# Sample attention and half of the conditioning slices moved into the output projection, two counts of the bit search moved to ScalarE

## The chip, the cores and the metric

One core of one Trainium2 chip runs the whole program. Its engines are TensorE (PE), VectorE (DVE), ScalarE (ACT), GpSimd (POOL) and SyncE (SP), which only issues DMAs. Each engine works through its own instructions in the order of the program and waits on semaphores for the others. The metric is the device time of one execution in microseconds (us), lower is better.

## The reference

One inference step of a two-layer decoder trunk on 1024 prompt tokens and 8 sequences of 4 sample tokens, T = 1056 columns of D = 1024 features. Layer 0 is sparse attention, layer 1 a short convolution; each has a SwiGLU feed-forward, and every sub-layer a norm whose shift, scale and gate come from a conditioning vector (`mod = silu(c) @ ada_w + ada_b`). What matters here:

```python
q, k, v, qi, ki, wi = attn_project(h, w_in, pos)          # 16 query heads, 4 key heads of 64
sc = indexer_scores(qi, wi, ki, valid)                    # one score per query token and key
_, sel = lax.top_k(sc, topk)                              # 256 keys (prompt), 129 (sample)
o = sparse_attend(q, take_rows(k, sel), take_rows(v, sel), valid)   # softmax over those alone
yp = yp + g1p * (o @ w_o)                                 # then norm 2 and the feed-forward
```

The sample tokens attend to 512 cached keys, read through a page table (4 pages of 128 for each sequence), and to their own 4.

## The kernel before

**Numbers.** Products are made to fp32 accuracy from three passes: a weight tile is split into `uhi` (ACT, `split_hi` L294, `proj_hi` L731) and `ulo` (POOL, `split_lo` L301, `proj_lo` L737), and `up_product` (L313, matmuls on L309) issues 24 matmuls for 128 output features and one chunk of CH = 352 columns; I call this an item. Three chunks cover T.

**Loads.** Weights come through `wraw`, a ring of WR = 4 slots of 512 KB, in one fixed order. SP issues them; each waits until the slot's last user is done (`ring_wait` L636).

**Stages.** (a) Norm 1, the indexer's projections, and the index scores for query tiles 2 to 7 of 128 tokens and for the sample (to 197.5 us); tile i sees 128 (i + 1) keys, so the rows of scores are 384 to 1024 long. (b) `pe_proj_b`, the other projections in 39 items, with rotations (`pe_rot` L747) and K and V turned to tokens (ACT L937). Into these items all 80 chunks of conditioning weights `ada_w` are woven: `pe_chunks` L754, matmuls on L765, a chunk being 512 KB, one ring slot; eight chunks make a slice, which ACT takes to `qstage` (L782) and `mod` (L788). In the meantime DVE runs `dve_select` (L1369): the k-th largest score of every row by a binary search over the 32 bits of a float. Each of 32 iterations counts, for six tiles and the sample, the scores at or over a candidate (`count`, L1383), and makes the next candidate with small steps in two groups (`small` L1416; L1419, L1421, L1423, L1425). (c) Sample attention, `pe_att_s` L1525 with its ACT, DVE and SP parts: eight batches in a software pipeline, K and V pages of a batch loaded by SP with a table read each (L1223 to L1233), keys turned (L1480), scores with mask (L1488, L1492), probabilities turned (L1500), values (L1514). DVE also makes the masks of the six tiles from the thresholds there (`dve_mask` L1455, seven instructions each, one of them a scan, L1466). (d) Prompt attention, `pe_att` L1662: 64 pairs of heads, tile by tile, three pairs ahead; PE scores L1629, DVE adds the mask and takes the extreme (L1686), ACT exponentiates (L1729), POOL scales (L1764), PE turns (L1640, L1645) and multiplies with the values (L1658), DVE and ACT copy. (e) Output section, `pe_out` L1807: 24 items with the gate and the residual added by DVE (L1868), and norm 2's sums of squares (`pe_add`, L345) and its application between them; then the feed-forward, whose first half units belong to the window shown below.

**SP's order around the change:** the stores of q, the 16 DMAs of output weights 0 to 3 (`sp_out_w`, L1782), the pages of the sample, the q tiles of prompt attention, then the reload of y (L1787, 4.2 MB) and the other output weights.

**PE's order** is the list of calls:

```python
            pe_proj_b(pe)
            pe_att_s(pe)
            pe_att(pe)
            pe_out(pe)
            pe_ffn(pe, "ffn0", 1, 2)
```

## Time and profile before

| | us |
|---|---|
| median of 3 runs | 2957.48 |
| lowest, highest | 2954.46, 2960.81 |
| the profiled execution | 2959.58 |
| its span in the trace | 2957.2 |
| (b) projections and selection | 257.0 |
| (c) sample attention | 108.4 |
| (d) prompt attention | 250.6 |
| (e) output section, with twelve half units of the feed-forward | 163.7 |

The four stages are windows of the trace, cut where PE's work changes; they touch, from 197.5 to 977.2 us. PE is busy for 2784.2 us of the span (94%), DVE for 1266.0, ACT for 788.4, POOL for 879.3. A row of windows gives for a stretch the busy time and the number of instructions of each engine, then TensorE's granted clock as a share of the full 2.4 GHz, the busy share of the DMA engines and what they moved. A row of a timeline gives start, duration, engine, line, operation, output and inputs; in square brackets the idle time ahead of it and what ended it. SPq stands for SP's issue of DMAs.

### The profile page before, as it was taken

How to read it: one execution, taken by the hardware profiler on the slowest of the kernel's cores; microseconds unless marked ns; L12 is line 12 of the kernel's file. 1: busy time of each engine (PE TensorE's matmuls, PEld its weight loads, DVE VectorE, ACT ScalarE, POOL GpSimd, SP SyncE). 2: the span in 40 equal slices, each digit the busy share in tenths (PEclk: the TensorE clock that was granted, in tenths of full speed). 3: DMA queues.
4: the chain of work that ended last, by engine and by line, in shares of the span. 5: the costliest groups of instructions: out<-in, count | busy, mean ns of one | idle time of the engine just before them, and what ended most of it. 6: DMA issues, size and time to landing. Idle time of an engine off the chain costs nothing.

```text
span 2957.2 us, 46842 instructions
## 1 busy us (share of the span) xinstructions
PE 2784.2 (94%) x18034; PEld 2529.6 (86%) x18034; DVE 1266.0 (43%) x3043; ACT 788.4 (27%) x1488; POOL 879.3 (30%) x673
## 2 busy tenths in 40 slices
PE   5878895999999999999999989999799999999999
PEld 4746673557798999999999889999699999999999
DVE  6499998556614222222223253323432222222233
ACT  4151212387616111111111441111331111111113
POOL 3312442133315322232222342222242223223320
PEclk8999996599999999999999999999899999999999
DMA  8216654200041111111111111012011221111101
GB/s 291 77 44 207 211 190 140 65 23 16 2 130 29 43 43 43 43 43 43 43 43 43 43 48 53 15 57 58 1 43 49 59 60 45 43 43 43 43 15 60
DMA packets 207293, 191.17 MB, mean 65 GB/s; under 512 B 32176, under 2 KB 185368, under 8 KB 206906
## 3 DMA queue, kind: packets, MB, share of 16 engines
q1 hardware_dynamic: 207162, 189.38, 21.4%
q8 instruction: 88, 1.44, 0.2%
q14 instruction: 43, 0.35, 0.0%
HBM read 173.86 MB, written 15.48 MB: 64 GB/s over the span
## 4 chain that ended last, share of the span: by engine, by line
PE 84%; SPq 3%; DVE 3%; POOL 3%; DMA 2%; ACT 2%; issue 2%; DVEq 0%; ACTq 0%; POOLq 0%
PE PS L309 69%; PE PS L1629 3%; PE PS L1658 3%; PE PS L1640 2%; PE PS L345 2%; DVE s_all L1343 1%; DMA wraw<-in_ada_w_dram 1%; PE PS L765 1%; SPq L676 1%; POOL ulo L301 1%; ACT na L418 1%; PE PS L2332 1%; POOL hlo L430 1%; DVE na L394 1%; SPq L675 1%
## 5 line engine op out<-in xcount | busy, mean ns | idle before, releaser
L309 PE MATMUL PS<-hhi,uhi 128*128 128x352 f32 (+1 forms) x3240 | 1065.3, 329 | 27.8 <-DVE hlo L1117 10.4
L309 PE MATMUL PS<-hhi,ulo 128*128 128x352 f32 (+1 forms) x3240 | 1047.4, 323 | 0.0
L309 PE MATMUL PS<-hlo,uhi 128*128 128x352 f32 (+1 forms) x3240 | 1046.7, 323 | 0.0
L309 PEld LDWEIGHTS PS<-hhi,uhi 128*128 128x128 f32 (+1 forms) x3240 | 612.8, 189 | 50.0 <-issue 28.4
L309 PEld LDWEIGHTS PS<-hlo,uhi 128*128 128x128 f32 (+1 forms) x3240 | 614.5, 190 | 3.5 <-issue 0.2
L309 PEld LDWEIGHTS PS<-hhi,ulo 128*128 128x128 f32 (+1 forms) x3240 | 613.1, 189 | 0.8
L309 PE MATMUL PS<-ahi,dhi 128*128 128x352 f32 x1248 | 424.3, 340 | 26.7 <-DVE y L478 21.5
L2030 POOL TENSOR_TENSOR alo<-af,ahi 128x352 fp32r<-128x352 f32 x132 | 125.1, 948 | 1073.4 <-ACT ahi L1975 1073.4
L2077 DVE TENSOR_TENSOR af<-sg,PS 128x352 f32<-128x352 f32 x132 | 68.8, 521 | 872.9 <-PE PS L309 857.6
L309 PE MATMUL PS<-ahi,dlo 128*128 128x352 f32 x1248 | 404.8, 324 | 0.0
L309 PE MATMUL PS<-alo,dhi 128*128 128x352 f32 x1248 | 403.5, 323 | 0.0
L478 DVE SCALAR_TENSOR_TENSOR y<-PS,mod,y 128x352 f32<-128x352 f32 x416 | 242.7, 584 | 177.0 <-PE PS L309 177.0
L301 POOL TENSOR_TENSOR ulo<-wraw,uhi 128x1024 fp32r<-128x1024 f32 x120 | 285.3, 2400 | 69.6 <-ACT uhi L294 69.5
L309 PEld LDWEIGHTS PS<-ahi,dhi 128*128 128x128 f32 x1248 | 235.6, 189 | 57.1 <-DVE y L487 23.9
L1973 ACT ACTIVATE sg<-PS 128x352 f32<-128x352 f32 x132 | 61.3, 464 | 678.4 <-PE PS L309 678.3
L309 PEld LDWEIGHTS PS<-alo,dhi 128*128 128x128 f32 x1248 | 236.7, 190 | 3.8 <-issue 0.7
L309 PEld LDWEIGHTS PS<-ahi,dlo 128*128 128x128 f32 x1248 | 236.4, 189 | 0.0
L1975 ACT ACTIVATE ahi<-af 128x352 fp32r<-128x352 f32 x132 | 65.8, 498 | 500.5 <-DVE af L2077 500.5
L1764 POOL TENSOR_SCALAR Pb<-Pb,bv 128x128 f32<-128x128 f32 (+7 forms) x128 | 93.7, 745 | 238.2 <-DVE bv L1693 238.2
L1383 DVE TENSOR_SCALAR_CACHE_REDUCE junkA<-s_all,bv 128x1024 bf16<-128x1024 f32 (+4 forms) x162 | 162.6, 1004 | 1.4 <-DVE bv L1410 0.3
L481 DVE SCALAR_TENSOR_TENSOR y<-PS,mod,y 128x320 f32<-128x320 f32 x208 | 114.5, 551 | 55.5 <-PE PS L309 47.1
L294 ACT ACTIVATE uhi<-wraw 128x1024 fp32r<-128x1024 f32 x120 | 119.7, 1045 | 55.8 <-PE PS L309 27.1
(261 smaller groups left out, 2848.0 us busy)
## 6 DMA issues: line engine op xcount, KB each, us to landing
wraw<-in_ffn_w_gu_dram SPq DMA_DIRECT2D x88, 512.0 KB, 7.3
wraw<-in_ada_w_dram SPq DMA_DIRECT2D x80, 512.0 KB, 4.7
draw<-in_ffn_w_down_dram SPq DMA_DIRECT2D x44, 512.0 KB, 4.3
wraw<-in_conv_w_in_dram SPq DMA_DIRECT2D x24, 512.0 KB, 7.1
adaw<-in_ada_w_dram SPq DMA_DIRECT2D x16, 512.0 KB, 12.6
y_scratch<-y SPq DMA_DIRECT2D x1, 4224.0 KB, 12.5
q_scratch<-kiB SPq DMA_DIRECT2D x24, 176.0 KB, 3.8
y<-y_scratch SPq DMA_DIRECT2D x1, 4224.0 KB, 13.2
```

The costliest lines, as they stand in the source:

```text
L294: act.activation(uhi[:, u % WR, :, 0:cols], wraw[:, slot, :, 0:cols], ACT.Copy).then_inc(up_hi, 1)
L301: pool.tensor_tensor(ulo[:, u % WR, :, 0:cols], wraw[:, slot, :, 0:cols], uhi[:, u % WR, :, 0:cols].bitcast(F32), ALU.subtract).then_inc(u ...
L309: last = pe.matmul(out, w(kt), x(kt), start=(n == 0), stop=(n == 3 * count - 1))
L478: dve.scalar_tensor_tensor(out=y[:, m, chunk(n)], in0=b[:, 0:CH], scalar=gate(m)[:, 0:1], in1=y[:, m, chunk(n)], op0=ALU.mult, op1=ALU.add ...
L481: dve.scalar_tensor_tensor(out=y[:, m, 2 * CH:SEQ], in0=b[:, 0:PC], scalar=gate(m)[:, 0:1], in1=y[:, m, 2 * CH:SEQ], op0=ALU.mult, op1=ALU ...
L1383: return dve.tensor_scalar(junk(j, rows, L), s, at, 0.0, ALU.is_ge, ALU.add, accum_out=one(cnt, j)[0:rows])
L1629: last = pe.matmul(wide(2 * g)[:, c], q_of(i)[64 * g:64 * g + 64, t, :], kT[64 * g:64 * g + 64, t // 4, c], start=True, stop=True)
L1658: last = pe.matmul(bank[6 + n % 2][64 * g:64 * g + 64, 0:P], v_tok[:, j, 64 * kv:64 * kv + 64], PT[:, n % 2, g, j * P:j * P + P], start=(j ...
L1764: pool.tensor_scalar(p, p, bv[:, at:at + 1], 1.0, ALU.mult, ALU.mult).then_inc(p_nrm, 1)
L1975: act.activation(ahi[:, jj, chunk(n)], af[:, p, :], ACT.Copy).then_inc(act_hi, 1)
L2030: pool.tensor_tensor(alo[:, jj, chunk(n)], af[:, k % 2, :], ahi[:, jj, chunk(n)].bitcast(F32), ALU.subtract)\
L2077: dve.tensor_tensor(af[:, p, :], sg[:, p, :], bank[2 * p + 1][:, 0:CH], ALU.mult).then_inc(act_f, 1)
```

## The change

1. **ACT counts tiles 7 and 6** (1024 and 896 scores a row) with Sign and a sum, in `act_count`, one iteration in each of the items 2 to 33, on semaphores `cand_rdy` and `sign_cnt`. DVE counts the other five and waits for `sign_cnt` ahead of the first small step. Because Sign sums +1, 0 and -1, a short refinement of the two thresholds follows the loop.
2. **40 of the 80 chunks** (`SG_W` = 5 slices of 10) stay in the projections; the gains that need the others are made behind the output section (`dve_gains_late`).
3. **Prompt attention follows the projections directly.** DVE makes the masks of the sample and of tile 2 first; the other five are cut in 30 steps, ahead of the pairs 0 to 27 (`dve_masks_at`). For tiles 0 to 3, q is loaded in two halves into free parts of `PT`. The splits of output weights 0 to 3 lie at pairs 6 to 19 on ACT and POOL.
4. **The output section is 20 slots and eight items.** The slots hold 16 items (none in slots 0, 5, 10, 15), the sample attention (batch c from slots 2c and 2c + 1 on, keys turned in two halves over one bank), 40 chunks in slots 0 to 14, and the output weights 4 to 7. K and V have two buffers in place of four. SP issues the pages of a batch in odd slots. y comes back in three parts. The last eight items take chunk 1 and 2 of the columns; for these the weights 0 to 3 are loaded and split again (`N_OUT` = 12). Items use two banks (the last eight four) in place of six.

In the diff's core, "..." marks what is left out:

```diff
-N_SG = ADA1 // 8
+N_SG, SG_W = ADA1 // 8, 5
...
 def chunk_at(item):
-    return ADA1 * item // N_ITEMS
+    return 8 * SG_W * item // N_ITEMS
+
+
+def slot_chunks(s):
+
+    sg, r = divmod(s, 3)
+    lo = 8 * (SG_W + sg) + 3 * r
+    return range(lo, min(lo + 3, 8 * (SG_W + sg) + 8)) if s < 15 else range(0)
+
+
+TURN_AT = {4: 0, 6: 1, 10: 2, 12: 3, 16: 4}
...
+        def act_count(act, item):
+
+            i = item - 2
+            if not 0 <= i < 32:
+                return
+            act.wait_ge(cand_rdy, i + 1)
+            for j in range(NA):
+                L = L_OF[(7, 6)[j]]
+                act.activation(junkA[:, SEQ * j:SEQ * j + L], score((7, 6)[j]), ACT.Sign, bias=bv[:, CAND + j:CAND + j + 1],
+                               scale=-1.0, accum_out=bv[:, BS + j:BS + j + 1]).then_inc(sign_cnt, 1)
...
+        def sp_keys(sp, b):
+            sp.wait_ge(tpb_mm if b < 2 else kst_mm, turned_b(60, 1) if b < 2 else 2 * b - 2)
+            for g in range(NPG):
+                page = sp.value_load(bvi[0:1, 152 + 4 * b + g:153 + 4 * b + g], min_val=0, max_val=39)
+                sp.dma_start(Kr(b)[:, g, :], cache_k[0][bass.ds(page, 1)].rearrange("o p g d -> p (o g d)"))\
+                    .then_inc(ks_loaded[b % 2], 16)
...
+                    ins = dve.scalar_tensor_tensor(out=vi(cand, a, b), in0=vi(inc, a, b),
+                                                   scalar=bvi[:, bass.ds(i + (BITI + 1), 1)],
+                                                   in1=vi(th, a, b), op0=ALU.bitwise_or, op1=ALU.bitwise_or)
+                    if g == 0:
+                        ins.then_inc(cand_rdy, 1)
                     signal(dve.tensor_tensor(vi(th, a, b), vi(th, a, b), vi(inc, a, b), ALU.bitwise_or))
...
             with dve.Fori(0, 32) as i:
-                dve.wait_ge(sel, i * 8 + base)
-                count(first, None)
-                dve.wait_ge(sel, i * 8 + (base - 1))
+                dve.wait_ge(sel, i * 7 + base)
+                count(NA, None)
+                count(NA + 1, None)
+                dve.wait_ge(sign_cnt, i * NA + NA)
                 small(1, 0, i)
...
+            for j in range(NA):
+                s, rows, L, k = entries[j]
+                A = relu[:, j, 0:L]
+                link(dve, dve.tensor_scalar(A, s, one(th, j), -NEG, ALU.is_le, ALU.mult))
+                link(dve, dve.tensor_tensor(A, A, s, ALU.max))
+                link(dve, dve.tensor_reduce(one(cand, j), A, AX_X, ALU.min))
+                link(dve, dve.tensor_scalar(A, s, one(cand, j), 0.0, ALU.is_ge, ALU.add, accum_out=one(cnt, j)))
+            link(dve, dve.tensor_tensor(v(ge, 0, NA), v(cnt, 0, NA), v(kk, 0, NA), ALU.is_ge))
+            link(dve, dve.tensor_tensor(v(inc, 0, NA), v(ge, 0, NA), v(cand, 0, NA), ALU.mult))
+            link(dve, dve.tensor_tensor(v(th, 0, NA), v(th, 0, NA), v(inc, 0, NA), ALU.max))
...
+        def dve_masks_at(dve, entries, n):
+
+            for x in range(30 * n // 28, 30 * (n + 1) // 28 if n < 28 else 0):
+                dve_mask_step(dve, entries, (5, 4, 3, 1, 0)[x // 6], x % 6)
...
+                if n in (6, 10, 14, 18):
+                    split_hi(act, "out", (n - 6) // 4, MM0["out"])
...
+                if n in (7, 11, 15, 19):
+                    split_lo(pool, "out", (n - 7) // 4)
...
+        def sp_slot_chunks(sp, s):
+            for c in slot_chunks(s):
+                sp_chunks(sp, c, c + 1)
+
         def sp_out(sp):
+            sp_slot_chunks(sp, 0)
+            sp_keys(sp, 0)
+            sp_keys(sp, 1)
             sp.wait_ge(o_rdy, NPAIR)
-            sp.dma_start(y[:], y_scr).then_inc(y_back, 16)
-            for m in range(WR, KT):
-                sp_out_w(sp, m)
+            sp.dma_start(y[:, :, chunk(0)], y_scr[:, :, chunk(0)]).then_inc(y_back, 16)
+            sp.dma_start(repa[:], k_rep_a).then_inc(rep_loaded, 16)
+            sp.dma_start(qS[:], q_scr[:, :, SEQ:T]).then_inc(qs_loaded, 16)
+            sp_values(sp, 0)
+            sp_values(sp, 1)
+            for n in (1, 2):
+                sp.dma_start(y[:, :, chunk(n)], y_scr[:, :, chunk(n)]).then_inc(y_back2, 16)
+            for s in range(N_SLOT):
+                if s:
+                    sp_slot_chunks(sp, s)
+                if s in (1, 3, 6, 8):
+                    sp_out_w(sp, WR + (1, 3, 6, 8).index(s))
+                if s % 2 and (s + 3) // 2 < NB:
+                    sp_keys(sp, (s + 3) // 2)
+                if s % 2 and 2 <= (s - 1) // 2 < NB:
+                    sp_values(sp, (s - 1) // 2)
+            for w in range(KT, N_OUT):
+                sp_out_w(sp, w)
...
+        def pe_out_item(pe, k):
+            m, n = out_item(k)
+            w = m if k < 20 else KT + m
+            if k < 8 and n == 0 or 8 <= k < 12 or k >= 20:
+                pe.wait_ge(up_lo, UP0["out"] + w + 1)
+            if k < 18:
+                after(pe, yo_upd, k - 1)
+            elif k < 20:
+                pe.wait_ge(ss_exp, NB)
+            else:
+                pe.wait_ge(yo_upd, k - 3)
+            if k == 16:
+                pe.wait_ge(so_lo, NB)
+            up_product(pe, out_bank(k)[:, 0:CH], (UP0["out"] + w) % WR, n).then_inc(up_mm, 1)
+
+        def pe_slot_chunks(pe, s):
+
+            for c in slot_chunks(s):
+                sg, kt = divmod(c, 8)
+                n = A_RING[c]
+                pe.wait_ge(w_loaded[n % WR], 16 * (n // WR + 1))
+                if c == 8 * SG_W:
+                    pe.wait_ge(c32_rdy, 4)
+                if kt == 0:
+                    pe.wait_ge(ada_stg, G0 + sg)
+                for b in range(4):
+                    last = pe.matmul(bank[5][32 * b:32 * b + 32, 0:256], cT32b[:, kt, :],
+                                     wraw[:, n % WR, 2 * b:2 * b + 2, :].rearrange("p a x -> p (a x)"),
+                                     start=(kt == 0), stop=(kt == KT - 1))
+                last.then_inc(ada_mm, 1)
...
         def pe_out(pe):
             pe.wait_ge(o_rdy, NPAIR)
...
+            for s in range(N_SLOT):
+                if s in OUT_SLOTS:
+                    pe_out_item(pe, OUT_SLOTS.index(s))
+                c = s // 2
+                if s % 2 == 0:
+                    if c < NB:
+                        smp_turn_k(pe, c, 0)
+                    if 0 <= c - 1 < NB:
+                        smp_scores(pe, c - 1)
+                    if 0 <= c - 2 < NB:
+                        smp_turn_p(pe, c - 2)
+                else:
+                    if c < NB:
+                        smp_turn_k(pe, c, 1)
+                    if 0 <= c - 2 < NB:
+                        smp_values(pe, c - 2, G0 + SG_W + len([t for t in TURN_AT if t < s]))
+                pe_slot_chunks(pe, s)
+                if s in TURN_AT:
+                    pe_slot_turn(pe, s)
+                for j in SUM_AT.get(s, ()):
+                    pe_add(pe, 1, 0, j)
+            for k in range(16, 24):
+                pe_out_item(pe, k)
+                for j in range(2 * (k % 4), 2 * (k % 4) + 2) if k < 20 else range(k - 20, k - 19):
+                    pe_add(pe, 1, 1 if k < 20 else 2, j)
...
             pe_index_s(pe)
             pe_index(pe)
             pe_proj_b(pe)
-            pe_att_s(pe)
             pe_att(pe)
             pe_out(pe)
             pe_ffn(pe, "ffn0", 1, 2)
```

The first place is ACT's order in the projections, in the middle of the 39 items. L892 and L899 take a projection tile and its rotated rows, L731 splits a weight, L782 takes a slice. Before:

```order
L892 ACTIVATE psgB<-PS 128x352 [waits qc_rdy,rot_mm,up_mm]
L899 ACTIVATE pafB<-PS 128x352 [waits fin_rdy,rot_mm]
L731 ACTIVATE uhi<-wraw 128x1024 [waits up_mm,wq_loaded2,w_loaded2]
L782 ACTIVATE qstage<-PS 128x256 [waits ada_turn,ada_mm]
L892 ACTIVATE psgB<-PS 128x352 [waits qc_rdy,rot_mm,up_mm]
L899 ACTIVATE pafB<-PS 128x352 [waits fin_rdy,rot_mm]
```

After, where L953, L960, L780 and L831 are these four, and L849 is the count:

```order
L953 ACTIVATE psgB<-PS 128x352 [waits qc_rdy,rot_mm,up_mm]
L960 ACTIVATE pafB<-PS 128x352 [waits fin_rdy,rot_mm]
L780 ACTIVATE uhi<-wraw 128x1024 [waits up_mm,wq_loaded3,w_loaded3]
L849 ACTIVATE junkA,bv<-s_all,bv 128x1024 [waits cand_rdy]
L849 ACTIVATE junkA,bv<-s_all,bv 128x896
L831 ACTIVATE qstage<-PS 128x256 [waits ada_turn,ada_mm]
```

Two counts, of 1024 and 896 columns, have come between, each pair waiting for DVE's candidate.

The second place is PE's order around one sample batch. Before, in the sample stage, with L1480 the turn of keys, L1488 and L1492 the scores, L1500 and L1501 the turn of the probabilities, L1514 and L1517 the values:

```order
L1480 MATMUL PS<-ident,smpb 128x128 x8
L1488 MATMUL PS<-s_smp,repa 128x512
L1492 MATMUL PS<-smpb,qSr 16x512 x4
L1488 MATMUL PS<-s_smp,repa 128x4
L1492 MATMUL PS<-smpb,qSr 16x4 x4
L1500 MATMUL PS<-ident,smpb 128x128 x4
L1501 MATMUL PS<-ident,smpb 4x128
L1514 MATMUL PS<-PTs,smpb 64x16 x8
L1517 MATMUL PS<-PTs,vnew 64x16 x2
L1514 MATMUL PS<-PTs,smpb 64x16 x8
L1517 MATMUL PS<-PTs,vnew 64x16 x2
L1480 MATMUL PS<-ident,smpb 128x128 x8
```

After, in the slots 4 and 5 of the output section; L1621 and L1622 turn probabilities, L1944 is the chunks, L1955 the turn of a slice, L1596 half of the keys, L1636 and L1639 the values, L355 the output items:

```order
L1621 MATMUL PS<-ident,Ps 128x64 x4
L1622 MATMUL PS<-ident,Ps 4x64
L1944 MATMUL PS<-wraw,cT32b 32x256 x12
L1955 MATMUL PS<-ident,ada_stg 128x128 x2
L1596 MATMUL PS<-ident,Kr 128x128 x4
L1636 MATMUL PS<-PTs,Vr 64x16 x8
L1639 MATMUL PS<-PTs,vnew 64x16 x2
L1636 MATMUL PS<-PTs,Vr 64x16 x8
L1639 MATMUL PS<-PTs,vnew 64x16 x2
L1944 MATMUL PS<-wraw,cT32b 32x256 x8
L355 MATMUL PS<-hhi,uhi 128x352
```

Three chunks stand between a batch's first and second half, two more ahead of the next item.

The third place is SP's order behind the values of one batch. Before:

```order
L1230 TENSOR_LOAD bv
L1230 ISA x2
L1231 ISA
L1231 DMA smpb<-in_cache_v_dram 128x256
L1233 DMA vnew<-out_dram 4x256
L1223 TENSOR_LOAD bv [waits kst_mm]
L1223 ISA x2
L1224 ISA
L1224 DMA smpb<-in_cache_k_dram 128x256
```

After, where L1317 and L1321 load the values, L706 a chunk and L1876 an output weight:

```order
L1316 TENSOR_LOAD bv
L1316 ISA x2
L1317 ISA
L1317 DMA Vr<-in_cache_v_dram 128x256
L1321 DMA vnew<-out_dram 4x256
L706 DMA wraw<-in_ada_w_dram 128x1024 [waits up_lo]
L706 DMA wraw<-in_ada_w_dram 128x1024 [waits ada_mm]
L1876 DMA wraw<-in_attn_w_out_dram 64x4x128 [waits ada_mm]
L1876 DMA wraw<-in_attn_w_out_dram 64x4x128 x3
L706 DMA wraw<-in_ada_w_dram 128x1024 [waits ada_mm] x3
```

Before, the next batch's keys followed the values at once; now two chunks, an output weight and three more chunks stand between, each waiting for a slot of the ring.

## Rows read from the trace of the kernel before

**Rows 1.** windows by stage: from:to, length, busy us PE PEld DVE ACT POOL, clock, DMA, GB/s
```profile
197.50:454.50 257.00, 227.27 (x1674) 180.97 (x1674) 255.26 (x723) 46.92 (x107) 100.72 (x96) 0.93 0.62 196
454.50:562.90 108.40, 77.21 (x584) 46.19 (x584) 79.68 (x158) 22.62 (x54) 11.75 (x7) 0.56 0.41 113
562.90:813.50 250.60, 245.53 (x2112) 161.55 (x2112) 144.35 (x449) 178.21 (x448) 93.72 (x128) 0.92 0.05 14
813.50:977.20 163.70, 156.94 (x913) 148.25 (x914) 46.17 (x83) 59.44 (x101) 57.81 (x42) 0.98 0.25 72
...
563.00:603.00 40.00, 37.09 (x164) 19.20 (x164) 14.08 (x86) 24.28 (x98) 11.30 (x28) 0.50 0.06 14
603.00:650.00 47.00, 46.91 (x386) 27.41 (x386) 25.87 (x102) 40.42 (x117) 20.34 (x34) 1.00 0.12 30
```

**Rows 2.** DVE's timeline at the start and end of the bit search
```profile
215.59 1.01 DVE L1383 TENSOR_SCALAR_CACHE_REDUCE junkA<-s_all,bv 128x768 bf16<-128x768 f32 x1 [0.26 <-DVE bv L1410]
...
455.27 1.26 DVE L1383 TENSOR_SCALAR_CACHE_REDUCE junkA<-s_all,bv 128x1024 bf16<-128x1024 f32 x1
...
462.07 1.26 DVE L1383 TENSOR_SCALAR_CACHE_REDUCE junkA<-s_all,bv 128x1024 bf16<-128x1024 f32 x1
...
463.27 2.29 DVE L1419 TENSOR_TENSOR bv<-bv 128x4 f32<-128x4 f32 x1
...
471.23 5.15 DVE L1452 TENSOR_SCALAR s_all<-s_all,bv 128x1024 f32<-128x1024 f32 x6
```

**Rows 3.** SP's timeline from the end of the projections on
```profile
456.89 10.59 SPq L1782 DMA_DIRECT2D wraw<-in_attn_w_out_dram  x16
467.85 0.34 SPq L1217 DMA_DIRECT2D repa<-in_k_rep_a_dram  x1
...
483.82 3.67 SPq L1224 DMA_DIRECT2D smpb<-in_cache_k_dram  x4
...
493.27 3.64 SPq L1224 DMA_DIRECT2D smpb<-in_cache_k_dram  x4
```

**Rows 4.** ACT's timeline, the sample's exponentials
```profile
490.19 0.69 ACT L1588 ACTIVATE smpb<-PS,bv 128x516 f32<-128x516 f32 x1 [3.37 <-DVE bv L1560]
```

**Rows 5.** instructions of L1419 from 219 to 456: durations in ns
```profile
L1419 DVE TENSOR_TENSOR bv<-bv x60: 145/157/2322, 220.8 to 451.9; 128x4 f32<-128x4 f32 x30, 128x3 f32<-128x3 f32 x30
```

**Rows 6.** ACT's timeline around the tokens of K
```profile
305.76 0.46 ACT L892 ACTIVATE psgB<-PS 128x352 f32<-128x352 f32 x1 [9.51 <-PE PS L309]
...
322.26 0.46 ACT L892 ACTIVATE psgB<-PS 128x352 f32<-128x352 f32 x1 [4.28 <-PE PS L309]
```

**Rows 7.** PE's timeline at the end of the projections
```profile
450.85 0.32 PE L309 MATMUL PS<-hhi,ulo 128*128 128x352 f32 x1
...
451.70 1.50 PE L765 MATMUL PS<-wraw,cT 128*32 128x256 f32 x24
```

**Rows 8.** DMA issues from 472 to 565: count, KB, median us to landing
```profile
qbuf<-q_scratch SPq DMA_DIRECT2D x2, 512.0 KB, 5.1
```

**Rows 9.** groups of DVE by line, 482 to 563: busy us, mean ns
```profile
L1466 DVE TENSOR_TENSOR_SCAN relu<-relu 128x384 f32<-128x384 f32 (+5 forms) x6 | 9.8, 1626 | 0.2
...
L1464 DVE TENSOR_SCALAR bv<-bv 128x1 f32<-128x1 f32 x6 | 0.9, 153 | 0.2
```

**Rows 10.** the page's groups by line, POOL's weight split
```profile
L301 POOL TENSOR_TENSOR ulo<-wraw,uhi 128x1024 fp32r<-128x1024 f32 x120 | 285.3, 2400 | 69.6 <-ACT uhi L294 69.5
```

**Rows 11.** PE's timeline in the sample attention
```profile
489.33 1.70 PE L1480 MATMUL PS<-ident,smpb 128*128 128x128 f32 x8
...
493.58 0.66 PE L1500 MATMUL PS<-ident,smpb 128*128 128x128 f32 x4
```

**Rows 12.** the chain of waits, 340 to 352: start, us, what
```profile
344.73 3.69 DMA wraw<-in_ada_w_dram
```

**Rows 13.** windows in the projections, columns as in group 1
```profile
366.00:368.00 2.00, 0.00 (x0) 0.00 (x0) 2.00 (x7) 0.00 (x0) 1.79 (x2) 0.94 0.91 317
368.00:370.00 2.00, 1.68 (x10) 0.88 (x11) 2.00 (x6) 0.00 (x0) 0.00 (x0) 0.50 0.98 360
```

619 lines of the change are left out of this document (349 added, 270 removed).

## The prediction

> **What bounds the kernel now.** I read first the windows of the trace, one per stage [rows 1]. The projections with the selection (197.5 to 454.5) keep DVE busy for 255.26 of 257 us and PE for 227: DVE's bit search spans the stage. In the sample attention (454.5 to 562.9, 108.4 us) PE is busy for 77 us at a granted clock of 0.56; no engine is full, its work waits on hand-overs. Prompt attention (250.6 us) and the output section (163.7 us: output projection, norm and the first half units of ffn0) keep PE at 98 and 96%. Next, DVE's timeline in the bit search: the first count starts at 215.59, the loop ends at 471.23, so 255.6 us for 32 iterations, 7.99 each; one that POOL does not disturb takes 462.07 - 455.27 = 6.80 [rows 2]. Then SP's timeline: how long it takes to issue what comes in its order [rows 3].
>
> **The change, part by part.** The sum has three terms: when prompt attention starts, how long it lasts, and what the output section costs. All behind them is the same.
>
> *1. Start of prompt attention, now 562.9.* The loop on DVE loses the counts of two tiles, 1920 columns, at 1.20 us per 1024 (455.27 to the next instruction, with its read-out) 2.26 us. ACT takes these two as Sign with a sum. Nothing in the trace is that operation; the nearest is the Exp with a sum over 516 columns, 0.69 us [rows 4]: by columns 2.6 us for both; bounds 2.0 and 3.0. It starts when DVE has made the candidate and runs beside two of DVE's counts (some 1.5 us), behind which DVE waits; with the small steps now back to back I put 0.34 us on all this, so an iteration is 6.80 - 2.26 + 0.34 = 4.88, and 32 are 156 us. POOL's delays are measured as a sum: 32 x (7.99 - 6.80) = 38 us. A small two-operand step of DVE takes 0.145 us at best and 2.32 at worst [rows 5]; the one at 463.27 took 2.29. POOL's work in these items is unchanged, so I keep 38 (bounds 10, if the delays fall into DVE's new wait for ACT, and 50, since POOL's share of the time rises from 39 to 50%). One thing is new: ACT works in order, so the tally of an iteration is queued behind an item's evacuations. Where ACT also moves the K tokens it needs 322.26 - 305.76 = 16.5 us from one item to the next [rows 6], against some 6.3 for an iteration; the loop loses about 9, less 2 of POOL's delays that fall in it: 7. Loop: 156 + 38 + 7 = 201 us, end at 416.6.
>
> Behind the loop DVE has the refinement of two tiles (eight passes over 1024 or 896 columns, 9 us by the counts' price), the sign products (5.15 and 0.5 [rows 2]) and the masks of the sample and of one tile (some 8): ready at about 440. PE's side is later. ACT's last tally is asked for 3 us ahead of the loop's end, at 413.6; of the five items without a tally PE has run two ahead, and a bit under three remain at 4.5 us: 424.5. From there SP's order is as before: stores of q, the sixteen DMAs of the output weights, 467.85 - 450.85 = 17 us after the last product's last matmul [rows 3, 7], then the first q, 5.1 us from issue to landing [rows 8]. Start: 424.5 + 17 + 5 = 446.5, or **-116.4** (bounds -144 and -104, by POOL's delays). The 40 chunks that leave the projections (20 us of PE) count nothing there: DVE's loop covers them, and without that cover they would bring up to 20.
>
> *2. Prompt attention, now 250.6.* DVE gets the other five masks. Six tiles cost 34.9 us over seven lines, first and last in [rows 9]; without tile 2, 31. They come in the first 28 pairs. There, in the 87 us from 563 to 650, DVE is busy for 14 + 26 = 40 us [rows 1], so 31 fit on the average. But a step of up to 2.6 us stands in DVE's order ahead of copies that PE waits for. Bounds: 5 (nearly all in DVE's gaps) and 30 (all of it on the path). I take the middle, **+16**. The four weight splits on ACT and on POOL (2.4 us each there [rows 10]) stand beside ACT's 65 and POOL's 32 of 87 us, and are in it.
>
> *3. Output section, now 163.7.* Its last twelve half units of ffn0 are some 46 us before and after, so 118 us stand before them: 24 items at 4.0 (24 matmuls of 156.94 / 913 = 0.17 us [rows 1]) are 96, the rest is sums and the reload of y. After, there are 20 slots and then eight items. The slots hold 16 items (65 us), 40 chunks (1.50 us for three [rows 7], so 20), and eight sample batches at about 4.5 us (turns and scores 493.58 - 489.33 = 4.25 at full clock [rows 11]): 121 us if nothing waits. That is the floor.
>
> What waits is in SP's order. In an odd slot SP waits for PE's turn of the keys, then issues four key and four value pages with their table reads, 493.27 - 483.82 = 9.45 us [rows 3], and only behind these the next even slot's chunks. In the kernel before only the sample stage itself stood behind those pages. A chunk takes 3.69 us from issue to landing [rows 12], each next one 1.6 more (512 KB at the 317 to 360 GB/s of full queues [rows 13]). PE takes its instructions in order: it stands at the even slot's chunks until they land, and the turn that frees SP comes behind them, in the next odd slot, after an item. The two-slot loop is closed: 9.5 + 3.7 + 3.2 + 0.5 (last chunk) + 4.0 (item) + 0.8 (turn) = 21.7 us, with 13 to 15 us of PE work in it. Six of them, slot 3 to slot 15, are 130. Ahead of slot 3 stand y's parts, two small loads, ten value DMAs and seven chunks: 34 us. Slots 15 to 19 hold four items (16), eight sums (3) and the last batches with hand-overs (12): 31. Slots together 195 us (bounds 165, if pages issue in 0.6 us each and land beside the chunks, and 206, if a chunk needs 2.2 instead of 1.6). Items now use two banks, not six: each waits for the add two back, 0.5 us behind 4 us of product, hidden unless DVE stands at a sample step; that is in the hand-overs.
> Then items 16 to 23: 8 x 4.0 + 12 sums at 0.45 = 38, and 2 for the last tiles at ffn0's start. 195 + 38 + 2 = 235 against 118: **+117** (+87 to +128). The weights of tiles 0 to 3 are loaded and split a second time for the third chunk of columns; these four splits on POOL, 9.6 us, lie beside the 38.
>
> Sum: -116.4 + 16 + 117 = +16.6 on the profiled execution, whose own time is 2959.58 (span 2957.2), 2.1 above the median of the three runs, 2957.48. So 2957.48 + 16.6 = **2974**.
>
> **A rule against the trace.** DVE's small two-operand step takes 0.145 or up to 2.32 us, and the long one at 463.27 stands beside a POOL instruction of the 2.4 us kind [rows 2, 5, 10]; the counts, with one tile as input, keep their 1.2.
> The Trainium skill (SBUF — State Buffer, section "SBUF: two separate sides") calls the port pair shared by DVE and GpSimd an exclusive lock, held for a whole instruction.
> By that rule, the trace agrees, the delays go by the number of collisions, not by the length of the iteration; a delay in proportion to the time would be 30 us instead of 38, and the sum 2966.
>
> **Rivals.**
> *A. The slots overlap.* If chunks are issued before PE needs them, a two-slot period is what SP has to issue (9.5 of pages, 5.3 chunks at 0.4, half an output weight 1.3: 13) or what PE has to do, 15 us at most. For it: four ring slots stand ready. Against: SP's order puts eight pages ahead, and they wait for PE. Six periods 6.7 us shorter: **2934**, the faster side. It decides where SP's wait for the turn ends a slot earlier than PE needs the chunks behind it.
> *B. POOL's delays vanish in the wait for ACT.* Delay 10, not 38, start 28 earlier: **2946**.
> *C. Attention stays at half clock to pair 28.* From 563 to 603 the granted clock is 0.50, from 603 on 1.00 with PE busy all 47 us [rows 1]. If DVE's mask steps leave PE with gaps, that second stretch runs at half clock: +23, **2997**.
> *D. The clock falls in the slots.* After 2 us and more without a matmul the granted clock stood at 0.50 (1.2 GHz) [rows 13]. The closed loop has such waits; the item, chunk and turn behind one (5.3 us) then take twice as long, six times 5: **3004**. Against it: a chunk's matmuls cut most of the waits.
> The Trainium skill (TensorE: Matmul & The Clock Gate, section "HAM oscillation — how this bites in real kernels") describes this pattern, bursts of matmuls between waits for DMA that bring the clock down each time; the trace agrees at one place, 366 to 370 us.
>
> **How the numbers follow.** The forecast, 2974 (own range 2960 to 2988), has 0.42; A 0.20, B 0.14, C 0.12, D 0.12. Low 2932: half of A is left out. High 2999: C is in, most of D out. A difference of 0.2%, 5.9 us, is about what a measurement can tell from none. Faster by more: A, two thirds of B, 0.05 of the forecast's tail: 0.34. Within: the rest of B and 0.07 of the forecast: 0.12. Slower: 0.54.
>
> **What would show it.** The first score matmul of prompt attention near 446; under 430 is B. DVE's loop at 6.3 us an iteration, its wait for ACT under 1 us. Attention 262 to 270 us long; C is a clock of 0.50 far past its first 40 us. In even slots PE waits 3 to 6 us for chunks whose issue stands behind SP's pages, and odd slots start some 21.7 us apart; near 15 is A. A granted clock near 0.9 in the slots; near 0.5 is D. The forecast is wrong if pages or softmax hand-overs, and not chunks, end PE's waits, or if y's reload holds the first items for over 5 us.

## The result, and the profile after

The change made the kernel slower: 2999.25 us as the median of four runs (2989.07 to 3010.48) against 2959.14 for the kernel before (2954.46 to 2970.44), a ratio of 1.0116 with a 95% interval of 1.0086 to 1.0147 (the quotient of the two medians, 1.0136, lies in the interval). The profiled execution of the changed kernel took 2989.07 us, the shortest of the four. Its difference from the profiled one of before is 29.5 us where the medians differ by 40.1; the terms below are read from it, so they account for 29.5 us and not for the rest. By the ratio, 2957.48 us become 2992: within the stated range of 2932 to 2999, but above the forecast's own range of 2960 to 2988, and the loss of some 34 us is twice the 16.6 of the sum; on the profiled executions it is 29.5 against 16.6.

The windows of the changed kernel, with the columns of [rows 1]. The first three answer to its stages (the sample stage is gone as a stage), the next two split the third into slots and last items, then come pairs of attention that ran at full clock before, and the middle of the slots:

```profile
197.50:444.60 247.10, 204.09 (x1343) 164.51 (x1341) 222.23 (x663) 112.24 (x225) 105.64 (x98) 0.91 0.44 133
444.60:710.90 266.30, 244.55 (x2112) 160.59 (x2112) 176.50 (x489) 181.25 (x452) 106.31 (x132) 0.93 0.08 23
710.90:1006.50 295.60, 240.53 (x1851) 198.45 (x1852) 79.46 (x144) 79.13 (x163) 68.48 (x46) 0.89 0.45 139
710.90:914.60 203.70, 150.69 (x1339) 114.07 (x1339) 31.33 (x80) 25.56 (x71) 9.46 (x4) 0.85 0.57 176
914.60:960.50 45.90, 44.59 (x241) 40.92 (x242) 34.87 (x47) 32.83 (x57) 34.52 (x24) 0.96 0.34 104
484.00:531.00 47.00, 36.74 (x274) 20.28 (x273) 34.30 (x96) 31.64 (x94) 21.61 (x26) 0.95 0.05 12
735.00:870.00 135.00, 104.70 (x935) 76.46 (x935) 20.75 (x51) 17.08 (x45) 9.46 (x4) 0.82 0.60 187
```

Stage by stage, with the forecast's three terms:

| term | forecast | measured |
|---|---|---|
| start of prompt attention | 446.5 (-116.4) | 444.6 (-118.3) |
| length of prompt attention | 266.6 (+16) | 266.3 (+15.7) |
| output section | 280.7 (+117) | 295.6 (+131.9) |
| of it the 20 slots | 195 | 203.7 |
| of it what follows the slots, ahead of 46 us of ffn0 | 40 | 45.9 |

The DVE timeline of the changed kernel at both ends of the bit search: 209.76 is the first count, 412.36 the first instruction behind the loop, so 202.6 us or 6.33 an iteration, against 6.28 forecast. In the first iteration DVE waited 4.74 us for ACT; there is one more such wait in the loop, of 7.08 us.

```profile
209.76 0.61 DVE L1465 TENSOR_SCALAR_CACHE_REDUCE junkB<-s_all,bv 128x384 bf16<-128x384 f32 x1
...
216.05 0.18 DVE L1499 TENSOR_TENSOR bv<-bv 128x2 f32<-128x2 f32 x1 [4.74 <-ACT junkA L849]
...
412.36 0.16 DVE L1535 SCALAR_TENSOR_TENSOR bv<-bv 128x2 f32<-128x2 f32 x1
```

PE's first scores of prompt attention, with the wait ahead of them:

```profile
444.57 0.80 PE L1720 MATMUL PS<-kT,PT 64*128 64x128 f32 x4 [19.62 <-DMA PT<-q_scratch]
```

SP's timeline in the slots of the changed kernel, where [rows 3] showed a batch's pages with nothing but the next pages behind them:

```profile
775.19 3.66 SPq L1310 DMA_DIRECT2D Kr<-in_cache_k_dram  x4
779.62 3.98 SPq L1317 DMA_DIRECT2D Vr<-in_cache_v_dram  x4
...
784.05 1.30 SPq L706 DMA_DIRECT2D wraw<-in_ada_w_dram  x3
785.40 2.81 SPq L1876 DMA_DIRECT2D wraw<-in_attn_w_out_dram  x4
788.88 3.68 SPq L706 DMA_DIRECT2D wraw<-in_ada_w_dram  x3
797.72 3.66 SPq L1310 DMA_DIRECT2D Kr<-in_cache_k_dram  x4
...
806.23 0.82 SPq L706 DMA_DIRECT2D wraw<-in_ada_w_dram  x2
```

The pages start at 775.19, the chunks behind them are issued from 784.05 on, and the next pages start at 797.72: 22.5 us for two slots, 21.7 forecast. Read in the same way, from one start of key pages to the next, the periods between 757.77 and 844.52 are 17.4, 22.5, 22.4 and 24.4 us. The chain of waits has PE in the same place, first the wait for the transfer, then the item behind it:

```profile
727.62 11.09 DMA wraw<-in_ada_w_dram
...
739.84 6.42 PE PS L355 x24
...
784.93 6.57 DMA wraw<-in_ada_w_dram
...
792.54 3.82 PE PS L355 x24
...
806.62 5.40 DMA wraw<-in_ada_w_dram
...
813.15 5.66 PE PS L355 x24
...
830.36 6.08 DMA wraw<-in_ada_w_dram
...
838.19 4.98 PE PS L355 x24
```

Over the slots PE waited 47.1 us for chunks, in 19 places (its list of waits, from 710 to 915):

```profile
PE PS L1944 <- DMA wraw<-in_ada_w_dram: 47.1, 19, 16.4
```

### The profile page after: what moved, and what is told of

The parts are those of the page before. It is cut to its first block, busy times and chain, and to the rows that moved or that the text cites. A ratio compares the mean times of both kernels' runs of the same rounds, so it can differ in the third digit from the quotient of the medians.

```text
span 2987.4 us, 46953 instructions
## 1 busy us (share of the span) xinstructions
PE 2769.4 (93%) x18058; PEld 2517.3 (84%) x18058; DVE 1221.4 (41%) x2929; ACT 854.0 (29%) x1620; POOL 895.3 (30%) x677
## 4 chain that ended last, share of the span: by engine, by line
PE 76%; DVE 8%; issue 4%; SPq 4%; ACT 3%; POOL 2%; DMA 2%; DVEq 0%; ACTq 0%; POOLq 0%
PE PS L355 65%; PE PS L1720 2%; PE PS L1749 2%; PE PS L1731 2%; DMA wraw<-in_ada_w_dram 1%; DVE s_all L1424 1%; PE PS L394 1%; POOL ulo L347 1%; DVE na L443 1%; ACT na L467 1%; DVE junkA L1465 1%; POOL hlo L479 1%; SPq L725 1%; DVE junkC L1465 1%; DVE bv L1503 1%
## 5 line engine op out<-in xcount | busy, mean ns | idle before, releaser
L355 PE MATMUL PS<-hhi,uhi 128*128 128x352 f32 (+1 forms) x3240 | 1069.5, 330 | 29.5 <-DVE hlo L1178 10.5
L355 PE MATMUL PS<-hhi,ulo 128*128 128x352 f32 (+1 forms) x3240 | 1049.0, 324 | 0.0
L355 PE MATMUL PS<-hlo,uhi 128*128 128x352 f32 (+1 forms) x3240 | 1049.0, 324 | 0.0
L355 PEld LDWEIGHTS PS<-hhi,uhi 128*128 128x128 f32 (+1 forms) x3240 | 615.1, 190 | 56.6 <-issue 34.7
L355 PEld LDWEIGHTS PS<-hlo,uhi 128*128 128x128 f32 (+1 forms) x3240 | 616.2, 190 | 3.6
L355 PEld LDWEIGHTS PS<-hhi,ulo 128*128 128x128 f32 (+1 forms) x3240 | 614.5, 190 | 0.8
L355 PE MATMUL PS<-ahi,dhi 128*128 128x352 f32 x1248 | 425.1, 341 | 27.1 <-DVE y L527 21.5
L355 PE MATMUL PS<-ahi,dlo 128*128 128x352 f32 x1248 | 404.7, 324 | 0.0
L355 PE MATMUL PS<-alo,dhi 128*128 128x352 f32 x1248 | 403.7, 323 | 0.0
L347 POOL TENSOR_TENSOR ulo<-wraw,uhi 128x1024 fp32r<-128x1024 f32 x124 | 296.3, 2411 | 114.9 <-ACT uhi L340 114.8
L355 PEld LDWEIGHTS PS<-ahi,dhi 128*128 128x128 f32 x1248 | 236.0, 189 | 57.3 <-DVE y L536 24.4
L355 PEld LDWEIGHTS PS<-alo,dhi 128*128 128x128 f32 x1248 | 237.0, 190 | 4.1 <-issue 1.5
L355 PEld LDWEIGHTS PS<-ahi,dlo 128*128 128x128 f32 x1248 | 236.2, 189 | 0.0
L506 POOL TENSOR_TENSOR dlo<-draw,dhi 128x1024 fp32r<-128x1024 f32 x52 | 123.9, 2404 | 0.1
L479 POOL TENSOR_TENSOR hlo<-na,hhi 128x352 fp32r<-128x352 f32 (+1 forms) x72 | 72.0, 1001 | 168.2 <-ACT hhi L470 168.0
```

The costliest lines, as they stand in the source:

```text
L347: pool.tensor_tensor(ulo[:, u % WR, :, 0:cols], wraw[:, slot, :, 0:cols], uhi[:, u % WR, :, 0:cols].bitcast(F32), ALU.subtract).then_inc(u ...
L355: last = pe.matmul(out, w(kt), x(kt), start=(n == 0), stop=(n == 3 * count - 1))
L479: pool.tensor_tensor(hlo[:, ft, cols_of(n)], nbufs(q)[1][:, k % 2, 0:width(n)], hhi[:, ft, cols_of(n)].bitcast(F32), ALU.subtract).then_in ...
L506: pool.tensor_tensor(dlo[:, b, :], draw[:, b, :], dhi[:, b, :].bitcast(F32), ALU.subtract)\
```

## The experiments

The forecast held in its sign and gave half of the loss, so the runs ask whether its reasons hold: first the closed loop in SP's order, then what each of the other terms is made of, then whether a version without the loop beats both kernels. In the table "start" is PE's first score of attention; "slots" is the time from the start of the output section to the first square of norm 2, in slot 15, which every version has.

| kernel | start | slots to 15 | median | ratio to before (95%) |
|---|---|---|---|---|
| the change | 444.6 | 171.0 | 2999.25 | 1.0116 (1.0086 to 1.0147) |
| e1 all chunks ahead | 471.6 | 98.3 | 2956.40 | 0.9978 (0.9965 to 0.9991) |
| e2 pages later | 445.5 | 157.4 | 2980.03 | 1.0059 (1.0042 to 1.0076) |
| e3 plain pages | 446.3 | 148.1 | 2976.34 (one run) | |
| e4 DVE counts all | 470.7 | 169.8 | 3026.54 (one run) | |
| e5 masks ahead | 473.1 | 169.9 | 3013.24 (one run) | |
| f1 SP's order, all chunks ahead | 461.4 | 91.7 | 2939.26 | 0.9919 (0.9891 to 0.9948) |
| f2 SP's order, chunks as in the change | 433.4 | 149.4 | 2964.24 | 0.9998 (0.9983 to 1.0014) |
| f3 stores between chunks | 464.0 | 97.5 | 2937.21 | 0.9908 (0.9878 to 0.9938) |
| f4 late splits | 467.5 | 93.4 | 2931.47 | 0.9891 (0.9875 to 0.9907) |
| g1 filler | 445.2 | 174.4 | 3002.83 | 1.0129 (1.0110 to 1.0147) |
| g2 one chunk a slot | 440.6 | 150.9 | 2961.24 | 0.9991 (0.9978 to 1.0005) |
| h1 pages two slots later | 441.9 | 106.7 | 2918.99 | 0.9860 (0.9834 to 0.9885) |

For e4 and e5 the start is the score that follows DVE's first maximum; the first scores were issued from 418.7 and 445.2 on, and then PE waited 51 and 27 us for DVE.

Start and slots are read from one profiled execution each. With all chunks ahead the start is uncertain by some 6 us: up to it f1 and f4 are the same program, and they have 461.4 and 467.5. The kernel before was measured again beside each group of runs, with medians from 2957.49 to 2964.90, so versions are best compared by their ratios.

**e1: all chunks ahead.** Nothing of the 80 chunks is left in the slots.

```diff
-N_SG, SG_W = ADA1 // 8, 5
+N_SG, SG_W = ADA1 // 8, 10
```

> The changed kernel with all 80 chunks of conditioning weights back in the projections, none in the slots; the rest as changed. My theory: in the slots PE waits for chunks whose issue stands behind SP's eight pages. Without chunks the slots fall from 203.7 to about 125 us (16 items, eight batches, hand-overs). The projections take 20 us more of PE, but DVE's loop at 6.3 us an iteration covers an item of 5.1: start of attention at most 5 us later than 444.6. Total about 70 us under the changed kernel, 2930, so some 30 under the kernel before. Rival 1, the batch's hand-overs and pages bound the slots, chunks only fill them: slots stay over 175. Rival 2, the woven chunks are then on the projections' path: attention starts 15 to 20 us later, net gain 50.

The slots came as forecast, 72.7 us shorter. The start did not: attention began 27 us later, more than either case allowed, and the gain was 43 us and not 70. PE's and DVE's waits from 210 to 471 in this kernel:

```profile
DVE bv L1500 <- ACT junkA L849: 27.6, 10, 8.7
...
PE PS L814 <- DMA wraw<-in_ada_w_dram: 26.6, 11, 4.2
```

PE waited 26.6 us for chunks in its items, so ACT's evacuations came late, its counts with them, and DVE waited 27.6 us for ACT (11.8 in the change). The change had tied the bit search to PE's items, and 80 chunks in 39 items slow the items. This is read from the waits; it fits that with 64 chunks ahead (h1) DVE waited only 10.9 us there. Two more waits stood in this trace, both ended by SP's order: DVE's second item waited for y (and PE 10.5 us for DVE behind it), and PE for the first q behind 10.6 us of output weights.

```profile
762.26 0.58 DVE L2078 SCALAR_TENSOR_TENSOR y<-PS,mod,y 128x352 f32<-128x352 f32 x1 [14.52 <-DMA y<-y_scratch]
```

```profile
471.61 0.80 PE L1721 MATMUL PS<-kT,PT 64*128 64x128 f32 x4 [18.75 <-DMA PT<-q_scratch]
```

**e2: pages later.** Only the place of the pages in SP's order.

```diff
                 if s:
                     sp_slot_chunks(sp, s)
+                if s and s % 2 == 0:
+                    if (s + 2) // 2 < NB:
+                        sp_keys(sp, (s + 2) // 2)
+                    if 2 <= (s - 2) // 2 < NB:
+                        sp_values(sp, (s - 2) // 2)
...
-                if s % 2 and (s + 3) // 2 < NB:
-                    sp_keys(sp, (s + 3) // 2)
-                if s % 2 and 2 <= (s - 1) // 2 < NB:
-                    sp_values(sp, (s - 1) // 2)
```

> The changed kernel with one edit in SP's order: the eight pages of a batch are issued behind the next even slot's chunks, not ahead of them. My theory (closed loop turn, pages, chunks): the chunks of the even slot are no longer 9.5 us late, two-slot periods fall from 22.4 to about 18, slots from 203.7 to about 188, total -15. Rival, the transfer rate of the chunks or the ring of four slots sets the period: same within 5 us.

Slots 13.6 us shorter, total 19 lower (17 by the ratios). The same loads in another order, so the order costs that much at least. It isn't all: PE still waited 34.1 us (47.1 in the change), since now the next odd slot's chunks are behind the pages.

**e3: plain pages.** One DMA of fixed places for four pages, so a batch's sample attention works on other keys and values.

```diff
-            for g in range(NPG):
-                page = sp.value_load(bvi[0:1, 152 + 4 * b + g:153 + 4 * b + g], min_val=0, max_val=39)
-                sp.dma_start(Kr(b)[:, g, :], cache_k[0][bass.ds(page, 1)].rearrange("o p g d -> p (o g d)"))\
-                    .then_inc(ks_loaded[b % 2], 16)
+            sp.dma_start(Kr(b)[:], cache_k[0][4 * b:4 * b + 4].rearrange("o p g d -> p o (g d)"))\
+                .then_inc(ks_loaded[b % 2], 64)
...
```

The same is done for the values.

> The changed kernel with the four pages of a batch loaded by one DMA from a fixed place in the cache, without the page table: SP needs about 1.5 instead of 9.5 us for a batch, the bytes are the same (the sample's keys and values are then those of other pages). My theory: what costs is SP's issue time; periods fall from 22.4 to 17, slots from 203.7 to 180. Rival, transfers or hand-overs: under 5 us less.

SP's timeline in this kernel: the pages take it under 2 us now, with the same bytes.

```profile
778.68 0.46 SPq L1308 DMA_DIRECT2D Kr<-in_cache_k_dram  x1
779.18 0.51 SPq L1313 DMA_DIRECT2D Vr<-in_cache_v_dram  x1
...
799.34 0.41 SPq L1308 DMA_DIRECT2D Kr<-in_cache_k_dram  x1
...
815.52 0.41 SPq L1308 DMA_DIRECT2D Kr<-in_cache_k_dram  x1
```

Slots to 15 are 22.9 us shorter, as expected; the periods 20.7 and 16.2. So SP's issue time, not the bytes of the pages, is in the loop. It isn't all of the loop: some 8 us of issue less shortened a period by 3 us on the mean (18.7 against 21.7, from the first key pages to the last), and PE still waited 30.3 us for chunks (47.1 in the change). It is one run.

**e4: DVE counts all.** The bit search of the kernel before, in the changed kernel: `act_count` is not called, DVE counts seven, no refinement.

> The changed kernel with the bit search as before: DVE counts all seven, ACT none, no refinement behind the loop. My theory: an iteration is 8.0 us again and not 6.33, the loop ends 53 us later, less 12 of refinement, so attention starts some 41 us later than 444.6, at 486, and is as long as before, 266. Rival, that the start came earlier because 40 chunks left the items: attention starts less than 20 us later.

Between both cases: the start moved by 26 us. ACT's counts are worth that, and the other 92 of the 118 us come from the sample's stage no longer standing there. My 41 was too much because the loop was at 7.61 us an iteration here (214.1 to 457.67) and not at 7.99. With 40 chunks fewer PE's items run ahead; a part of the iterations then has no POOL work beside it. Why the loop is faster here is an argument from the order; it was not tested apart.

**e5: masks ahead.** All seven masks between the loop and attention.

```diff
-            for j in (6, 2):
+            for j in (6, 2, 5, 4, 3, 1, 0):
...
-                dve_masks_at(dve, entries, n)
```

> The changed kernel with all seven masks ahead of prompt attention, none in its pairs. My theory: DVE gets 31 us between the loop and attention, so attention starts DVE-bound, at 439.3 + 31 = 470, 25 us later than 444.6; without the steps attention takes 251 to 253 us and not 266.3, so the masks are what made it longer. Rival, the weight splits on ACT and POOL at pairs 6 to 19, or q in two halves, made it longer: attention stays over 260.

The time of each tile of prompt attention, from DVE's last subtraction of one tile to that of the next, for tiles 1 to 4 (5 to 7 take 37.2, 42.4 and 41.9 everywhere), with TensorE's granted clock in tile 1 (full speed is 1.00, 0.50 is 1.2 GHz):

| kernel | tile 1 | tile 2 | tile 3 | tile 4 | clock in tile 1 |
|---|---|---|---|---|---|
| before | 23.5 | 21.7 | 26.6 | 31.9 | 0.68 |
| the change | 27.3 | 29.0 | 29.1 | 31.9 | 0.87 |
| e5, masks ahead | 27.7 | 24.9 | 26.6 | 31.9 | 0.62 |
| f1 | 30.1 | 29.0 | 29.1 | 31.9 | 0.61 |
| g1, attention as in the change | 30.6 | 31.8 | 29.1 | 31.9 | 0.50 |
| f4, late splits | 27.3 | 24.8 | 29.1 | 32.1 | 0.59 |
| g2, late splits | 21.9 | 24.8 | 29.1 | 32.1 | 0.90 |
| h1, late splits | 25.8 | 24.8 | 29.1 | 32.1 | 0.65 |

Tile 1 spreads by several us with no edit of attention, and it goes with the granted clock. In the profiled change the clock was at 0.50 up to 475, 31 us into attention, and in g1, whose attention is the same program, up to some 507, 62 us into it. The window from 39.4 to 86.4 us behind the start, 484 to 531 in the first fence with a clock of 0.95, reads in g1:

```profile
484.60:531.60 47.00, 42.14 (x236) 22.54 (x235) 31.97 (x87) 29.18 (x85) 19.16 (x25) 0.69 0.05 12
```

Two rows of DVE's timeline in the change, the ends of tiles 1 and 2, from which the table has 527.95 - 499.00 = 29.0:

```profile
499.00 0.29 DVE L1800 TENSOR_TENSOR hlo<-PS,hhi 128x128 fp32r<-128x128 f32 x1 [2.17 <-ACT hhi L1835]
...
527.95 0.29 DVE L1800 TENSOR_TENSOR hlo<-PS,hhi 128x128 fp32r<-128x128 f32 x1 [0.55 <-ACT hhi L1835]
```

Neither case of the expectation holds alone: without the masks tile 3 is back at its 26.6, tile 2 only from 29.0 to 24.9, tile 1 not at all. Attention could start only 31 us of masks behind the loop and was some 7 shorter, counted from DVE's first maximum; the execution took 3013.24 us, 24 more than the profiled one of the change. What is left in tiles 1 and 2 is where the weight splits lie (pairs 6 to 19), which f4 tests.

**f1 and f2: SP's order at both ends.** Two edits in both kernels: the first two q tiles ahead of the output weights, and y ahead of the value pages. f1 has all chunks ahead; f2 has the chunks of the change and e2's order too.

```diff
-            for m in range(WR):
-                sp_out_w(sp, m)
             sp_att(sp)
...
             for i in range(8):
+                if i == 2:
+                    for m in range(WR):
+                        sp_out_w(sp, m)
...
-            sp_values(sp, 0)
-            sp_values(sp, 1)
             for n in (1, 2):
                 sp.dma_start(y[:, :, chunk(n)], y_scr[:, :, chunk(n)]).then_inc(y_back2, 16)
+            sp_slot_chunks(sp, 1)
+            sp_values(sp, 0)
+            sp_values(sp, 1)
             for s in range(N_SLOT):
-                if s:
+                if s > 1:
                     sp_slot_chunks(sp, s)
```

> All 80 chunks in the projections, and two further edits of SP's order: the first two q tiles are loaded ahead of the sixteen DMAs of output weights, and the three parts of y ahead of the value pages. Where all chunks were ahead, SP issued output weights for 10.6 us between the last store of q and the first q load, with PE waiting, and PE waited 10.5 us for y in the slots. If both waits are ended by SP's order alone, the total falls by 17 to 20 us under that kernel, to about 2937, 0.8% under the kernel before. Rival, behind the output weights the stores of q, and behind y the keys' copies, come just as late: under 6 us less.

> The changed kernel with 40 chunks in the slots as it is, and three edits of SP's order: first q tiles ahead of the output weights, y and slot 1's chunks ahead of the value pages, and a batch's pages behind the next even slot's chunks. Attention starts 10 us earlier, near 434, if PE's side was what waited (DVE is ready at 439.3, so only 5 may come through). Slots from 203.7 to some 180: the first 16.4 us wait to 6, periods of 18. Total -25 to -30 against the changed kernel, about 2970, still over the kernel before. Rival: the wait at slot 1 is by the transfer of y, 4 MB ahead of the chunks, and stays.

f1: start 10.2 us earlier, slots 6.6 shorter, total 17: two waits ended by order alone. SP's timeline in f1, to be read beside [rows 3]:

```profile
446.29 9.61 SPq L744 DMA_DIRECT2D q_scratch<-qst_  x3
457.52 2.02 SPq L1305 DMA_DIRECT2D PT<-q_scratch  x4
459.59 10.58 SPq L1880 DMA_DIRECT2D wraw<-in_attn_w_out_dram  x16
```

f2: start 11.2 us earlier for PE, of which 7 count, since DVE made its first maximum at 438.47 (445.51 in the change); slots 21.6 shorter, total 35 lower, which is more than forecast and just the time of the kernel before. The rival, y's transfer ahead of the chunks, holds in part: the wait for slot 1's chunks fell from 16.4 to 9.0 us and not to 6, and PE went on some 10 us after SP had begun to issue them at 712.55.

**f3: stores between chunks.** In f1's projections SP alternates a store of q with a chunk.

> As the kernel with all 80 chunks ahead and SP's order mended at both ends, with one more edit: in the projections a tile's three stores of q, each waiting for POOL's last step, alternate with chunk loads, where all three stood ahead of them. In the kernel with all chunks ahead PE waited 27 us for chunks there, behind stores of 8 us. Theory: this wait ends with the order, attention starts 10 to 15 us earlier than without the edit. Rival: ring slots come free too late in any order, under 4 us.

The rival: PE's wait for chunks there was 25.1 us and 25.9 in f1, the start is no earlier (464.0 against 461.4), and the medians are 2 us apart with intervals that overlap. So this wait isn't made by the order of the stores. What ends it is open.

**f4: late splits.** f1 with the four splits at pairs 36, 40, 44, 48 on ACT and one pair later on POOL.

```diff
-                if n in (6, 10, 14, 18):
-                    split_hi(act, "out", (n - 6) // 4, MM0["out"])
+                if n in (36, 40, 44, 48):
+                    split_hi(act, "out", (n - 36) // 4, MM0["out"])
```

> As the kernel with all chunks ahead and SP's order mended (median 2939), with the four splits of output weights on ACT and POOL moved from the pairs 6 to 19 of prompt attention to the pairs 36 to 49. In the changed kernel tiles 1 and 2 of attention take 27.3 and 29.0 us against 23.5 and 21.7 before; with all masks ahead they still take 27.7 and 24.9. Theory: the splits cost 7 to 8 of the 16 us by which attention grew, because POOL's 2.4 us stands in front of a pair's scaling; later pairs are longer and cover them: total -7. Rival: the later pairs, with ACT and POOL busier, lose as much: same within 3 us.

The total is 7.8 us lower by the medians (the intervals just overlap), and in the table of tiles 2.8 in tile 1 and 4.2 in tile 2, with 0.2 lost in tile 4. The part in tile 1 is uncertain, since the change with its early splits also has 27.3 there. In tile 2 the effect is clear: 24.8 in f4, g2 and h1, and 29.0 or more in every version that has early splits and masks. So of the 15.7 us by which attention grew, the splits made 4 at the least and some 7 by f4, and the rest goes with the masks.

**g1: filler.** 20 transposes of a constant into an idle bank ahead of the chunks of even slots.

```diff
+                if s % 2 == 0 and 2 < s < 15:
+                    k = len([x for x in OUT_SLOTS if x <= s]) - 1
+                    pe.wait_ge(yo_upd, k)
+                    for _ in range(20):
+                        pe.transpose(out_bank(k + 1)[:, 0:P], ident[:], ident[:])
```

> The changed kernel with 20 transposes (3 us of PE at full clock) of a constant into an idle bank ahead of the chunks in the even slots 4 to 14, where PE otherwise waits; their results are read by nobody. Theory D, sized by the trace: in the slots the granted clock was 0.82 on the mean and items behind a wait took 5 to 6.4 us and not 3.8; with PE busy through the wait the clock stays up, items take 3.8, the slots shrink from 203.7 by 5 to 9. Rival: the clock falls nevertheless, since 3 us do not fill waits of 6 to 8, or the fillers outlast the short waits: same or up to 8 us longer.

The window 735 to 870 in this kernel, to be read beside the last row of the first fence:

```profile
735.00:870.00 135.00, 105.24 (x932) 78.53 (x932) 19.95 (x49) 16.06 (x42) 9.47 (x4) 0.85 0.62 195
```

The clock rose only from 0.82 to 0.85, and the slots to 15 took 3.4 us more. The twenty transposes took 2.4 us, less than the long waits, and none stood ahead of the waits in slots 1, 3 and 5 (16.7, 3.2 and 5.4 us). Where the waits that a filler left were short, it did hold the clock. In the chain of waits of g1:

```profile
820.50 5.34 DMA wraw<-in_ada_w_dram
...
826.53 4.02 PE PS L355 x24
...
865.11 5.72 DMA wraw<-in_ada_w_dram
...
871.88 3.82 PE PS L355 x24
```

These are the items of slots 9 and 13, behind fillers and waits of PE of at most 1.4 us; in the change they took 5.66 and 5.39. Behind a filler and a wait of 5.4 us the item of slot 11 still took 5.00. So the run shows that shorter idle stretches bring the items back to 3.8 to 4.0 us, but not what the whole is worth, as the fillers cost their own time.

**g2 and h1: one chunk a slot, and then the pages behind them.** g2 is f4 with two slices in the slots, one chunk in each. h1 is g2 with the pages issued behind the ring loads of the next two slots.

```diff
-    sg, r = divmod(s, 3)
-    lo = 8 * (SG_W + sg) + 3 * r
-    return range(lo, min(lo + 3, 8 * (SG_W + sg) + 8)) if sg < N_SG - SG_W else range(0)
+    lo = 8 * SG_W + (s + 1 if s else 0)
+    return range(lo, lo + (1 if s else 2)) if s < 15 else range(0)
```

```diff
-                if s % 2 and (s + 3) // 2 < NB:
-                    sp_keys(sp, (s + 3) // 2)
-                if s % 2 and 2 <= (s - 1) // 2 < NB:
-                    sp_values(sp, (s - 1) // 2)
+                z = s - 2
+                if z > 0 and z % 2 and (z + 3) // 2 < NB:
+                    sp_keys(sp, (z + 3) // 2)
+                if z > 0 and z % 2 and 2 <= (z - 1) // 2 < NB:
+                    sp_values(sp, (z - 1) // 2)
```

> As the kernel above with the late splits, but with two of the ten slices (16 chunks) in the slots, one chunk in a slot and not three. In the changed kernel a chunk in the slots cost (203.7 - 130) / 40, about 1.8 us, and in the projections (471.6 - 444.6) / 40 = 0.7. Theory: one chunk a slot leaves SP and the ring time ahead of PE, so a chunk costs its 0.5 us of PE: slots 8 us longer, attention 11 us earlier, total -3 against the kernel above. Rival: any chunk behind a batch's pages waits: slots 20 us longer or more, total +10.

> As the kernel with one chunk a slot (16 chunks in the slots, median 2961), with one edit in SP's order: the eight pages of a batch are issued behind the ring loads of the next two slots, and not ahead of them. With one chunk a slot the loop of turn, pages, chunk stayed, at 21.6 us for two slots, so its cost hangs on what stands behind the pages, not on how many chunks there are. Theory: with the two loads ahead of the pages the loop is open; slot 15 is reached 105 to 110 us after the start of the output section and not 151, total -40, near 2920, 1.4% under the kernel before. Rival: ring slots come free no earlier, so SP waits for them ahead of the pages and delays the pages instead: total -15 or less.

g2 missed by far, also its rival: to slot 15 it took 57 us more than f4, where 8 or 20 were expected, attention began 27 us earlier, and the total is 30 higher and not 3 lower or 10 higher. SP's timeline in g2: with one chunk behind the pages, and not three, the period is as long as ever, 790.07 - 768.90 = 21.2 and 811.97 - 790.07 = 21.9 us.

```profile
768.90 3.67 SPq L1313 DMA_DIRECT2D Kr<-in_cache_k_dram  x4
773.35 3.63 SPq L1320 DMA_DIRECT2D Vr<-in_cache_v_dram  x4
...
777.43 0.35 SPq L705 DMA_DIRECT2D wraw<-in_ada_w_dram  x1
...
790.07 3.67 SPq L1313 DMA_DIRECT2D Kr<-in_cache_k_dram  x4
...
811.97 3.66 SPq L1313 DMA_DIRECT2D Kr<-in_cache_k_dram  x4
```

In h1 it is 763.74 - 750.23 = 13.5 and 774.41 - 763.74 = 10.7:

```profile
750.23 4.04 SPq L1313 DMA_DIRECT2D Kr<-in_cache_k_dram  x4
...
763.74 4.05 SPq L1313 DMA_DIRECT2D Kr<-in_cache_k_dram  x4
...
774.41 3.66 SPq L1313 DMA_DIRECT2D Kr<-in_cache_k_dram  x4
```

PE's wait for chunks in the slots of h1 is one, at their beginning (list of waits, 697 to 805); in g2 it was 37.2 us in 8 places by 850:

```profile
PE PS L1949 <- DMA wraw<-in_ada_w_dram: 8.5, 1, 8.5
```

h1 is the closed loop opened: the same chunks, pages and items as g2, 44 us less to slot 15, 42 us less in all by the medians (39 by the ratios), and the fastest version, 2918.99 us, 1.4% under the kernel before. Against f4, which has no chunk in the slots, its 16 chunks cost 13 us to slot 15 and attention begins 26 us earlier.

## Why the prediction was right, and where it was off

**Start of attention** (-116.4 forecast, -118.3 measured). The iteration came out at 6.33 us against 6.28. One error helped: the loop began 5.8 us earlier than assumed (209.76 and not 215.59), because the three counts ahead of it are gone too, which is in the diff and which I had overlooked. It ended 4.2 us earlier than forecast, and the tail of PE and SP was 2.3 us longer. That PE's side would end last, with the output weights ahead of q, was right: in f1 and f2 PE's first score moved by 10 to 11 us with their order. The K tokens, forecast at 9 us lost, put 15.2 us between two of ACT's counts where neighbours stand 5.6 apart, and DVE waited 7.08 us there. ACT's timeline and DVE's wait:

```profile
292.84 1.15 ACT L849 ACTIVATE junkA<-s_all,bv 128x1024 bf16<-128x1024 f32 x1 [3.40 <-DVE bv L1505]
...
298.40 1.15 ACT L849 ACTIVATE junkA<-s_all,bv 128x1024 bf16<-128x1024 f32 x1 [2.60 <-DVE bv L1505]
...
313.60 1.14 ACT L849 ACTIVATE junkA<-s_all,bv 128x1024 bf16<-128x1024 f32 x1
...
315.89 0.16 DVE L1499 TENSOR_TENSOR bv<-bv 128x2 f32<-128x2 f32 x1 [7.08 <-ACT junkA L849]
```

The loop's 202.6 us lie near the 201 of the sum, but two of its terms missed and made up for each other. POOL's delays can be added up from the trace: what the small steps took above the shortest of their kind is 38.3 us over the loop before, as forecast, and 31.7 after, where 36 were kept (38 less 2). DVE's waits for ACT, 4.74 us in the first iteration and 7.08 at the K tokens, are 11.8 in place of 9. The other 159 us are undisturbed iterations, 156 forecast.

Single small steps of DVE took up to 2.31 us in the loop (a step of five columns, 0.23 at its shortest), [rows 5] had 0.145 to 2.32. The Trainium skill (SBUF — State Buffer, section "SBUF: two separate sides") calls the pair of ports that DVE and GpSimd share an exclusive lock. The long steps agree with it. That the delays go by the number of collisions and would therefore stay at 38 is not borne out: 31.7 is nearer to the 30 of delays in proportion to the time, and e4, with 26.4 us in a loop of 243.6, fits neither.

**Attention** (+16 forecast, +15.7 measured). The size was a middle between two bounds, so its hit is luck, and of the execution too: with the same order in attention the stage took 266.3 us here, 269.5 in e2 and 272.5 in g1. The parts are known roughly: about 7 us the weight splits (4 at the least), about 8 the masks. The step that failed is the term put at nothing: I had counted the splits as covered by the idle shares of ACT and POOL, and that was wrong. An average share of 37% does not cover a 2.4 us instruction that stands ahead of a scaling of 0.5 us which PE waits for.

**Output section** (+117 forecast, +131.9 measured). The mechanism was right: waits ended by chunks behind the pages, and SP's issue time, not the bytes, in the loop (e2, e3, h1). The six periods also came out as summed. By PE's timeline slot 3 begins at 749.17 and slot 15 at 879.53, so 130.4 us, 130 forecast, 21.7 a period on the mean. The 8.7 us that the slots took more than 195 lie outside the loop.

Ahead of slot 3 stand 38.3 us and not 34. PE waited 16.4 us for slot 1's chunks, whose transfer took 11.09 us in the chain of waits, behind the second and third part of y, and the walk had 3.7 for it; f2 shortened this wait by SP's order. The slots 15 to 19 took 35.1 us and not 31: the eight sums were 5.8 us and not 3 (four pairs of 1.45), and PE waited 3.7 us for ACT's squares.

Inside the loop errors cancel. In the chain of waits five items behind long waits took 6.42, 4.97, 5.66, 4.98 and 5.39 us and not 3.82, together 8.3 more, four of them in the loop (5.7), at a mean granted clock of 0.82. That is case D in a mild form, one item in a period at part of the clock and not item, chunk and turn. Other parts of the loop were as much shorter than summed; the period of 17.4 us is one. The Trainium skill (TensorE: Matmul & The Clock Gate, section "HAM oscillation — how this bites in real kernels") describes bursts of matmuls that each start at the low clock after a wait for DMA, and here the trace agrees for these five.

Behind the slots stand 45.9 us and not 40. The eight items with their twelve sums end at 955.5, so they took 40.9 and not 38: the first ran at a granted clock of 0.69 and took 5.5 us, and the next three came each 5.05 us, 4.1 of item and 0.9 of two sums. PE was busy for 44.59 of the 45.9 us, so it is their bound, as summed. The rest of the window is the first half unit of ffn0, which the forecast had in its 46 us.

**The rivals.** A, overlap, did not occur in the change, but it is what h1 does, with one chunk a slot: there the period is 10.7 to 13.5 us. B, POOL's delays at 10 us, fell: they were 31.7. C, half clock far into attention, did not occur in the profiled execution: from 484 to 531 the clock was 0.95, and PE was busy for only 36.7 of those 47 us (46.9 before), so there it was the waits and not the clock. But it comes in part with other executions of the same order: in g1 the clock was 0.69 in that window, and tiles 1 and 2 took 62.4 us and not 56.3. The four executions of the change spread over 21 us, and this may be a part of it; only one of them has a trace. D came in part.

**The size of the whole.** The three terms give +29.3 on the profiled execution. Of the 12.7 us that the sum missed, 14.9 are the output section's, less 1.9 and 0.3 in the other two. Differences were not forecast better than totals: -15 against -13.6 in e2's slots and -40 against -42 in h1 were near, g2's -3 against +30 was not. The walk holds where it counts the loop, and fails where it takes a load to be ahead of PE without counting what stands ahead of that load.

## What to carry to other kernels

Work woven into gaps is cheap only if its loads are issued ahead of whatever the loading queue must wait for; look in the queue's order for a wait that the consumer itself must end, and count the loop: wait, issue, landing, consumer, and back. The number of loads behind such a wait hardly matters (three or one: 21 to 24 us a period in most), their place does (10.7 to 13.5 us with one load a slot ahead of the pages). A share of idle time does not cover a long instruction that stands in order ahead of a short one on the path. And one trace is one execution: with the same order of attention tiles 1 and 2 took from 56.3 to 62.4 us, so an effect of a few us there needs more than two traces.

## What was not expected of the hardware

A page with a table read costs SP 0.91 us (3.66 for four) and a plain load of all four 0.41 to 0.51 (e3); eight pages are 9.5 us in which the queue issues nothing else. ACT's count of 1024 columns with Sign took 1.15 us and its read-out 0.19, that of 896 columns 1.03, within the bounds taken from the Exp. Twenty transposes ahead of the chunks of six slots left TensorE's granted clock at 0.85 (g1), while in f4 and h1, without the long waits, it was 0.97 and 0.94 from 697 to 849. At the start of attention it stayed at 0.50 for 31 us in the change and for some 62 us in g1, with the same order of instructions.
